# Causal attention inside a decoder step: score steps taken in groups of two blocks of 512 keys, with their values matmuls in one run

## What is computed

```
def fox_block(q, k, v, fq, fk, q_pos, k_pos):
...
    s = jnp.einsum('bqhd,bkhd->bhqk', q, k, preferred_element_type=jnp.float32) * ATTN_SCALE
    s = s + (jnp.transpose(fq, (0, 2, 1))[..., :, None] - jnp.transpose(fk, (0, 2, 1))[..., None, :])
    mask = k_pos[None, :] <= q_pos[:, None]
    s = jnp.where(mask[None, None], s, -jnp.inf)
    p = jax.nn.softmax(s, axis=-1)
    return jnp.einsum('bhqk,bkhd->bqhd', p.astype(v.dtype), v)
```

## Time and profile before

| | |
|---|---|
| runs (us) | 3807.77, 3808.41, 3811.89 |
| the profiled execution, its own time | 3809.71 us |
| its span, first to last instruction | 3808.1 us (1.6 us lie outside) |
| TensorE busy | 3488.4 us, 92% |
| VectorE, ScalarE, GpSimd busy | 1710.7, 1174.9, 1196.8 us |
| mean granted TensorE clock | 0.951 of full speed |
| attention's main part | 1180 to 2722 us of the span |

### The profile page before, as it was taken

The page is one execution under the profiler, slowest core; times in us unless marked ns, Lnnn a source line. Parts: engine busy times, 40 slices in busy tenths (PEclk is TensorE's granted clock), DMA queues, the critical chain, the costliest instruction groups (busy, mean ns, idle before and its releaser), DMA issues. The chain is left out here.

```text
span 3808.1 us, 52765 instructions
## 1 busy us (share of the span) xinstructions
PE 3488.4 (92%) x18932; PEld 2413.4 (63%) x18932; DVE 1710.7 (45%) x2708; ACT 1174.9 (31%) x1611; POOL 1196.8 (31%) x1146
## 2 busy tenths in 40 slices
PE   7999999796966999999999999999799999978998
PEld 5777777672814555656565656565367777757887
DVE  3222221251516556555655555555244353445554
ACT  4221221040314445454545454554410000000110
POOL 0000000133333566666666666666500000000000
PEclk9999999796977999999999999999899999989999
DMA  4222332399884121212121212100212111136765
GB/s 147 96 93 102 119 110 78 137 353 353 295 323 99 25 45 34 45 34 45 34 45 34 46 34 45 34 17 12 85 54 77 44 44 55 55 101 186 207 212 163
DMA packets 215996, 392.36 MB, mean 103 GB/s; under 512 B 60135, under 2 KB 102120, under 8 KB 213775
## 3 DMA queue, kind: packets, MB, share of 16 engines
q1 hardware_dynamic: 195079, 322.22, 27.2%
q0 software_dynamic: 20768, 68.17, 4.8%
HBM read 288.50 MB, written 101.99 MB: 103 GB/s over the span
## 5 line engine op out<-in xcount | busy, mean ns | idle before, releaser
L928 DVE TENSOR_REDUCE at_max_parts<-at_mx 128x1 f32<-128x512 f32 (+3 forms) x1152 | 731.4, 646 | 498.3 <-PE at_mx L997 428.9
L802 POOL TENSOR_TENSOR at_pair_sum<-at_probs 128x1024 f32<-128x1024 f32 x224 | 532.0, 2375 | 428.5 <-ACT at_probs L852 428.5
L852 ACT ACTIVATE at_probs<-at_st,at_gap 128x1024 f32<-128x1024 f32 x448 | 497.5, 1112 | 526.9 <-PE at_st L1029 525.9
L1049 PE MATMUL at_o_ps<-at_probs,at_v 128*64 128x512 f32 (+3 forms) x2304 | 544.9, 584 | 0.0
L1028 PE MATMUL at_st<-at_q_all,at_k_all 128*128 128x512 f32 (+3 forms) x1152 | 477.4, 414 | 0.0
L997 PE MATMUL at_mx<-at_k_one,at_q_top 67*128 67x512 f32 (+3 forms) x1152 | 454.0, 395 | 8.7 <-DVE at_max_parts L928 5.9
L1029 PE MATMUL at_st<-at_q_one,at_k_one 67*128 67x512 f32 (+3 forms) x1152 | 439.6, 382 | 0.0
L1028 PEld LDWEIGHTS at_st<-at_q_all,at_k_all 128*128 128x128 f32 x1152 | 218.5, 190 | 225.9 <-ACT at_probs L852 108.7
L93 PE MATMUL ga_acc<-ga_h_high,ga_w_high 128*128 128x512 f32 x768 | 312.3, 407 | 22.5 <-DVE ga_h_low L1293 21.0
L94 PE MATMUL ga_acc<-ga_h_low,ga_w_high 128*128 128x512 f32 x768 | 308.7, 402 | 0.0
L95 PE MATMUL ga_acc<-ga_h_high,ga_w_low 128*128 128x512 f32 x768 | 308.4, 402 | 0.0
(11 more groups left out here) (302 smaller groups left out, 4974.5 us busy)
## 6 DMA issues: line engine op xcount, KB each, us to landing
dc_pages<-in_cache_k_dram SPq DMA_DIRECT2D x128, 256.0 KB, 6.0
dc_pages<-in_cache_k_dram POOLq DMA_DIRECT2D x128, 256.0 KB, 5.7
dc_pages<-in_cache_v_dram SPq DMA_DIRECT2D x128, 256.0 KB, 7.1
dc_pages<-in_cache_v_dram POOLq DMA_DIRECT2D x128, 256.0 KB, 5.7
pj_x<-in_x_prompt_dram SPq DMA_DIRECT2D x32, 512.0 KB, 3.7
scratch_h_t<-pj_h_t SPq DMA_DIRECT2D x8, 2048.0 KB, 9.9
at_q_raw<-scratch_q_t SPq DMA_DIRECT2D x128, 128.0 KB, 3.0
at_k_raw<-scratch_k_t SPq DMA_DIRECT2D x64, 256.0 KB, 4.1
```

What stands on the lines that cost most here:

```text
L802: chain.link(nc.gpsimd.tensor_tensor(pair, first, second, ALU.add))
L852: nc.scalar.activation(probs[:, s % RING], st[:, s % 2], ACT.Exp, bias=bias).then_inc(exp_done, 1)
L928: nc.vector.tensor_reduce(max_parts[:, b % AHEAD, t, c:c + 1], mx[:, bank_of["unit", k] % 2, 0:width], AX_X, ALU.max).then_inc(bank_done, 1)
L1049: last = nc.tensor.matmul(o_ps[half * HD:(half + 1) * HD, b % 2, at:TILE], v[:, h % 2, 4 * c + own], probs[:, s % RING, half, at:TILE], st ...
```

## The change

Two quads form a **group** (144 of them, `NGROUP`). TensorE does, for each group: all four steps' scores with up to nine units at fixed places (`units_after(g, place)`: one ahead of the first half, one behind each half; seven in most groups with a diagonal quad), then the `spread_shift` of every block that starts in the next group, then the four `weigh` in a row, then the `total` of blocks that ended a group ago. The shift row goes into a bank of `st`, free once the exponentials of step 4g + 2 are done, and no longer into `mx`. A planner (`units_by`) places units so that those a spread needs lie at least two units (`LATE`) ahead of it; VectorE takes `combine` right behind the last needed unit. Block rounding on ScalarE comes whole behind a group's exponentials, one q or one k at most per group. `q_one` has three slots in place of two, `q_raw` and its kin seven in place of six, `shift_w` and `max_moved` two, `pair_sum` one. 24 units in place of 12 stand ahead of the first scores.

```
-    AHEAD = 6
-    EARLY = 3 * TT
+    AHEAD = 7
+    QONE = 3
+    LATE = 2
...
+    def most_units(g):
+        return 7 if g >= quad_base[NT] // 2 and (on_diagonal(2 * g) or on_diagonal(2 * g + 1)) else 9
+
+    units_by = [0] * NGROUP
+    for g in reversed(range(NGROUP)):
+        if starting(g + 1):
+            units_by[g] = unit_base[starting(g + 1)[-1] + 1] + LATE
+        if g + 1 < NGROUP:
+            units_by[g] = max(units_by[g], units_by[g + 1] - most_units(g + 1))
+        units_by[g] = min(units_by[g], unit_base[NB])
+    EARLY = units_by[0] - most_units(0)
...
+            for g in range(NGROUP):
+                for b in (ending(g - 1) if g >= 1 else []):
+                    copy_o(b)
+                for s in range(4 * g, 4 * g + 4):
+                    exps(s)
+                for b in starting(g + 1):
+                    copy_shift(b, starting(g + 1)[0])
+                for b in round_q_in.get(g, []):
+                    round_q(b)
+                for n in round_k_in.get(g, []):
+                    round_k(n)
...
-                    last = nc.tensor.matmul(mx[0:HD + 1, n % 2, t * P:(t + 1) * P], shift_w[:, t], ident_r[:], start=True, stop=True)
+                    last = nc.tensor.matmul(st[0:HD + 1, 0, b - first, t * P:(t + 1) * P], shift_w[:, b % 2, t], ident_r[:], start=True, stop=True)
...
-            for n in range(NQUAD):
-                b = block_of[n]
-                for s in (2 * n, 2 * n + 1):
-                    for half in range(2):
-                        scores(s, half)
-                        for k in units_after(s, half):
-                            unit(k)
-                    if s == last_step[b] and b + 1 < NB:
-                        spread_shift(b + 1)
-                if n >= 1:
-                    weigh(2 * n - 1)
-                weigh(2 * n)
-                for d in den_after(n):
-                    total(d)
-            weigh(NSTEP - 1)
+            for g in range(NGROUP):
+                for k in units_after(g, 0):
+                    unit(k)
+                for place in range(8):
+                    scores(4 * g + place // 2, place % 2)
+                    for k in units_after(g, place + 1):
+                        unit(k)
+                if starting(g + 1):
+                    pe.wait_ge(exp_done, 4 * g + 3)
+                for b in starting(g + 1):
+                    spread_shift(b, starting(g + 1)[0])
+                for s in range(4 * g, 4 * g + 4):
+                    weigh(s)
+                for b in dens_after(g):
+                    total(b)
```

More of the change, by code:

```diff
@@ L642, in phase_attend, with dens_after @@
-    for b, c in chunk_at.items():
-        for part in range(2):
-            round_k_at[first_step[b] + 2 + part] = (c, part)
-    low_k_at = {s + 1: c for s, (c, part) in round_k_at.items() if part == 1}
-    low_q_at = {last_step[b - 1]: b + 1 for b in range(1, NB - 1)}
+    def dens_after(g):
+        return ending(g - 1) if g >= 1 else []
+    bank_uses = [("unit", k) for k in range(EARLY)]
+    for g in range(NGROUP):
+        bank_uses += [("unit", k) for k in units_in(g)] + [("den", b) for b in dens_after(g)]
@@ new lines, in phase_attend, with free_group @@
+    bank_uses += [("den", b) for b in ending(NGROUP - 1)]
+    bank_of = {use: n for n, use in enumerate(bank_uses)}
+    round_q_in, round_k_in, busy = {}, {}, set()
+    def free_group(latest):
+        g = latest
+        while g >= 0 and g in busy:
+            g -= 1
+        busy.add(g)
+        return g
+    for n in reversed(range(2, H * NKC)):
+        h, c = divmod(n, NKC)
+        first = group_of_unit[unit_base[h * NT + 2 * c]]
+        if first >= 2:
+            round_k_in.setdefault(free_group(first - 2), []).append(n)
@@ new lines, in phase_attend @@
+    for b in reversed(range(NB)):
+        first = group_of_unit[unit_base[b]]
+        if first >= 2:
+            g = free_group(first - 2)
+            if g >= 0:
+                round_q_in.setdefault(g, []).append(b)
+    rounded_k = {n for ns in round_k_in.values() for n in ns}
+    rounded_q = {b for bs in round_q_in.values() for b in bs}
+    early_k = [n for n in range(H * NKC) if n not in rounded_k]
+    early_q = [b for b in range(NB) if b not in rounded_q]
+    group_of_k = {n: g for g, ns in round_k_in.items() for n in ns}
@@ new lines, in phase_attend @@
+    group_of_q = {b: g for g, bs in round_q_in.items() for b in bs}
+    low_k_in = {g + 1: ns for g, ns in round_k_in.items()}
+    low_q_in = {}
+    for b in range(NB):
+        if b not in early_q or b >= QONE:
+            low_q_in.setdefault(max(start_group[b] - 2, group_of_q.get(b, -1) + 1, 0), []).append(b)
+    for g, bs in round_q_in.items():
+        for b in bs:
+            assert end_group[b - AHEAD] <= g if b >= AHEAD else True, (b, g)
+            assert g + 1 < start_group[b]
+    for g, bs in low_q_in.items():
+        for b in bs:
+            assert g < start_group[b] and end_group[b - QONE] <= g, (b, g)
@@ L979, in bank_free @@
                 if n >= 2:
[L980 to L984 removed]
+                    pe.wait_ge(bank_done, n - 1)
             def unit(k):
@@ L1028, in scores @@
                 nc.tensor.matmul(out, k_all[h % 2][:, keys], q_all[:, b % AHEAD, at:TILE], start=True, stop=False)
-                last = nc.tensor.matmul(out, k_one[h % 2][0:KR, keys], q_one[0:KR, b % 2, at:TILE], start=False, stop=(c < j))
+                last = nc.tensor.matmul(out, k_one[h % 2][0:KR, keys], q_one[0:KR, b % QONE, at:TILE], start=False, stop=(c < j))
                 if c == j:
```

269 lines of the change are left out of this document (128 added, 141 removed).

## The result

The changed kernel takes **3789.95 us** (median of 5 runs, 3783.0 to 3794.4) against 3808.41 (5 runs): a ratio of **0.9949, 95% interval 0.9934 to 0.9964**. Faster, but by 18.5 us where 84 were forecast, and outside the range. The profiled execution took 3783.0, against 3809.7 before: -26.7. It is the fastest of the five, so what follows explains some 8 us more than the medians show.

A forecast was written before the change was run, and what follows sets the result against it. The prediction took TensorE to bound the attention phase (busy 1496 of 1542 us). Its terms, -50 - 72 + 33 - 7 + 11 + 1 = -84 against 3809.7, gave 3725.7, stated as 3724 us; range 3695 to 3775.

The forecast's parts named there:

- Seams: TensorE's switches from scores to values and back: 288 round trips become 144, at 0.35 us each, -50 us.
- Clock: Values that ran at 1.2 GHz behind late spreads cost about 13 us; half comes back, -7 us.
- Waits that go: TensorE's waits at diagonal quads and spreads, and for the copied shift, disappear: -72 us, bounds 40 and 91.
- new ones: Waits that replace the old: spreads and third-step scores late behind exponentials, spreads late behind `combine`; +33 us, bounds 10 and 60.
- Two of the new waits that I named: In groups with a diagonal quad: spreads behind third-step exponentials, 15.5 us; third-step scores behind the first step's, 16 us.
- GpSimd's adds: GpSimd's sums in the attention phase: claimed to take the same time, 995 of 1542 us busy.
- The narrow halves' 15: Diagonal quads' narrow halves, where units outpace their maxima: 0.25 us lost in each of 62 quads, to disappear, 15 us.
- Start: Ahead of the first scores: 24 units instead of 12, less units leaving the later stream; +11 us, bounds 8 and 16.
- ScalarE's rounding: Rounding of q or k moved behind a group's exponentials: has room there, costed at nothing.
- Waits as before, in new places: Spreads wait for exponentials, diagonal quads for ScalarE; only seams, start and end count: -38 us, 3770; chance 12%.
- VectorE sets the pace: Eight or nine maxima in a row with two banks slow units by 0.09 us each: +20 us, 3828; chance 8%.
- The signs: Profile checks: whole-quad groups 9.4 to 9.6 us, VectorE waits under 10; wrong if units over 0.72 apart or groups 9.7.

The follow-up runs named there:

- Experiment 6: The kernel before the change with 24 units ahead of its first scores in place of 12: 3810.29 us, ratio 0.9997.
- experiment 3: The changed kernel with the values matmuls of a group's last two steps moved into the middle of the next group's scores: 3845.19 us, ratio 1.0102.

## Why the prediction was wrong

The ledger follows my terms. First scores to last mask: -38.9; first scores later: +14.0; behind the phase: -1.7 (1088.1 to 1086.4). Sum -26.6, the 26.7 of the profiles.

- **Seams, -50: right.** Values and what is late ahead of them went from 546.9 to 505.8, -41. The seam's 0.35 stands in three rows: 0.09 ahead of the values and 0.15 in them, 35 us for 144 seams, and 0.11 at the second score behind them, another 16 in the row of scores. Together 51. By the Trainium skill (TensorE: Matmul & The Clock Gate, "What happens when you issue a matmul") I had worked out at most 0.16, and 23 for the term; the starts of both kernels show 0.35.
- **Clock, -7: nothing came back.** In the kernel before ten values stretches last longer than others of their widths, by 11.7 us together (my 13; nine stand behind a late spread, one behind a late unit). In the changed kernel there are nine, by 11.8 us. Without sums it is one (0.9), with halved sums two (2.2). So the clock followed the waits, and those did not go.
- **Waits that go, -72, and new ones, +33: the step that failed.** Together -39, and the ledger has +5 (134.1 late ahead of scores, units and spreads; 139.3 after). As 16 of the seams' 51 left these rows too, the waits themselves grew by about 21. Two of the new waits that I named are there, at no more than their price: 31 scores come 0.43 late behind exponentials (13 us for my 16), 17 spreads 0.29 (5 for 15.5). The third is where it failed: "In 16 of the 55 the last needed unit lies only two or three ahead of the spread, `combine` then takes 0.94", priced at 0.1 each, 1.5 in all. These 16 spreads came 1.0 to 1.5 us late, 19.9 in all, because `combine`'s add took up to 1.8 us there; without sums one such wait is left. The other failure is two sentences at a cost of nothing: "VectorE's rests of q and k stand behind a group's maxima, under the values too" and "GpSimd's adds take the same time". The rests do stand there, but so do GpSimd's adds, which before had mostly ended by then, and there `low_q` takes 1.50 for 0.95, `low_k` 2.51 for 1.27. Units that came over 0.2 late lost 32 us in 36 places, where before they lost 9 in 21 and without sums there are none. The row of `combine` with 0.76 at the earlier trace rows was the warning: 20 elements a partition in 0.76 us was no cost of its own but the stand-still (0.17 alone), and I carried the number forward as a constant.
- **The same term without sums.** In the changed kernel these places have 81.1, in the one before without sums about 120: some -40. Less the seams' 16 that is about -25, where I had -39.
- **The narrow halves' 15** I took back in full, and that is most of what is missing there. What came under 0.2 late behind a matmul narrower than 512 columns was 21 us before, 20 after and 18 without sums.
- **Start, +11: right.** From the last matmul of decode to the first score it is +14.9 (34.9 to 49.8), less 3.0 of pitch. Experiment 6 adds that for the kernel before the lead cost nothing in the end; how much of it the changed kernel got back wasn't separated.
- **ScalarE's rounding, nothing: right.** The waits view has none for it. **GpSimd's adds, "the same time": wrong,** the sum of 128x512 went from 1284 to 1389 ns on average, by standing still in its turn.
- **The rivals.** "Waits as before, in new places" comes nearest in kind, though its 3770 is 20 too low, and for another reason than I gave: exponentials are 18 us of it. "VectorE sets the pace" had the right engine, but the maxima ran at 690 ns and units stood 0.70 apart. It was the two-input instructions between them, 160 out of 1152 + 160, that were late.
- **The signs.** TensorE's waits for VectorE were to fall under 10 us; they are 46. Seven groups of two whole quads took 9.77 to 9.81 us, over the 9.7 that I had named as a sign of being wrong. That one misled: they hold nine units and two masks, for which 9.4 + 0.23 + 0.2 is about right. Units stood 0.70 apart, as forecast.

That the changed kernel with sums in quarters takes 3725, next to my 3724, is chance: VectorE still stands still for 40 us there. Without any of it the kernel takes 3711, and the change is then worth 71, not 84.

The ledger is of the fastest of five runs. The other four show a lower granted clock (0.945 to 0.948, against 0.949) and are 2 to 11 us slower; where they lose it, no trace shows.

## What to carry to other kernels

When a change moves work in time, list for each moved instruction not only what it waits for by semaphores but what runs beside it on the engine it shares a port with. A VectorE instruction that reads two tensors from SBUF next to GpSimd arithmetic costs its own time plus what is left of GpSimd's instruction. An instruction whose mean is far above its size (20 elements a partition in 0.76 us), or whose durations differ within one kernel, is the sign to look for. The remedy that gained most was to cut the *other* engine's long instructions in pieces (61 to 65 us); moving work away helped less (27), and cutting the blocked instruction in many short ones made it 227 us slower.

## What the runs showed of the hardware

- The stand-still is whole and goes both ways: VectorE's own time + (what is left of GpSimd's instruction - 0.13), within 0.02 us in all 124 of the changed kernel; GpSimd's 1.28 became 2.13 behind a `low_k`. Maxima from PSUM were never touched (690 ns inside a GpSimd instruction and outside).
- One tensor from SBUF with a scalar for each partition stands still as well: 0.84 us on average over all 288 instructions of 4 elements a partition, where one alone takes 0.22.
- A change from scores to values and back costs TensorE 0.35 us in this stream (0.39 in experiment 3, with some lower clock in it).
- Waits of 0.9 and 1.3 us, 5 us apart, were followed by a granted clock of 0.59 in the values; the values of the whole phase lost 10.7 of the 79 us that the sums cost that way. Not each such wait was followed by a lower clock.
